# Two-layer float32 block, layer one's experts: residual rows kept in HBM, their tile a seventh home for gate and up weights, up and down homes given out apart

## What is computed

```python
mix = hybrid_mixer(a_in, w_in[l], ...)
h = h + gt1[:, None, :] * mix                 # residual rows
m_in = modulate(rmsnorm(h, norm2_g[l]), sh2, sc2)
moe = hier_moe(m_in, w_router_grp[l], w_router_exp[l], w_gate[l], w_up[l], w_down[l])
h = h + gt2[:, None, :] * moe
return rmsnorm(h, normf_g)

def hier_moe(h, ...):                         # 32 experts, two chosen per token, hidden width 256
    def expert_step(acc, ws):
        wg, wu, wd, gate_col = ws
        y = (jax.nn.silu(hf @ wg) * (hf @ wu)) @ wd
        return acc + gate_col[:, None] * y, None
```

## Time and profile before

| | us |
|---|---|
| median of 3 executions | 1344.69 |
| the profiled execution, its own time | 1346.78 |
| span of its trace | 1345.0 |
| TensorE busy | 1285.8 (96%) |
| VectorE busy | 651.4 (48%) |
| ScalarE busy | 338.0 (25%) |
| GpSimd busy | 272.8 (20%) |

### The profile page before, as it was taken

How to read it: one execution, slowest core, us unless ns; L and a number is a source line. 1 busy time by engine, 2 the same in 40 slices (tenths; PEclk the granted TensorE clock), 3 DMA queues, 4 the chain that set the end, 5 groups by cost and what they waited for, 6 DMA issues and landing times. The chain is left out here.

```text
span 1345.0 us, 20902 instructions
## 1 busy us (share of the span) xinstructions
PE 1285.8 (96%) x8436; PEld 749.6 (56%) x8436; DVE 651.4 (48%) x1325; ACT 338.0 (25%) x578; POOL 272.8 (20%) x376
## 2 busy tenths in 40 slices
PE   7999999999998987999999999999999999999997
PEld 3555678865456322333388888888864633333332
DVE  7739767546665321222579996143544522111007
ACT  5422342524012100101345564111001211111113
POOL 4100530001000110110137547905300001010000
PEclk8999999999998988999999999999999999999999
DMA  9910011356647999999933211312135679999994
GB/s 372 375 64 1 1 63 64 128 220 219 256 170 264 409 425 420 424 423 424 393 145 111 77 63 63 124 64 78 59 132 248 245 291 360 420 392 421 391 410 188
DMA packets 43826, 316.00 MB, mean 235 GB/s; under 512 B 7256, under 2 KB 7264, under 8 KB 25040
## 3 DMA queue, kind: packets, MB, share of 16 engines
q1 hardware_dynamic: 35688, 296.34, 55.2%
q0 software_dynamic: 7584, 17.23, 3.4%
q10 hardware_dynamic: 456, 1.08, 0.2%
HBM read 302.11 MB, written 22.56 MB: 241 GB/s over the span
## 5 line engine op out<-in xcount | busy, mean ns | idle before, releaser
L2481 PE MATMUL m_ps<-store,par 128*32 128x512 f32 (+2 forms) x896 | 148.6, 594 | 0.0
L2481 PE MATMUL mix_ps<-store,par 128*32 128x512 f32 (+2 forms) x608 | 122.0, 636 | 17.2 <-issue 8.1
L2369 POOL DMA_INDIRECT y_t<-x_rows,m_token x25 | 25.5, 1019 | 452.6 <-DVE m_token L2355 199.1
L3197 PE MATMUL mix_ps<-y_t,store 128*128 128x256 f32 x432 | 96.2, 379 | 0.0
L2625 DVE TENSOR_TENSOR m2r_a<-m2r_a,m_ps 128x256 f32<-128x256 f32 x22 | 9.3, 421 | 170.7 <-ACT m2r_a L2546 170.7
L2481 PEld LDWEIGHTS m_ps<-store,par 128*32 128x32 f32 (+2 forms) x896 | 46.0, 119 | 81.2 <-issue 81.2
L3197 PEld LDWEIGHTS mix_ps<-y_t,store 128*128 128x128 f32 x432 | 82.1, 190 | 13.7 <-issue 2.6
L1284 PE MATMUL mix_ps<-y_t,store 128*128 128x512 f32 x192 | 85.6, 599 | 0.0
L2481 PEld LDWEIGHTS mix_ps<-store,par 128*32 128x32 f32 (+2 forms) x608 | 38.2, 129 | 79.9 <-issue 79.7
L2503 PE MATMUL m_ps<-store,m2r_a 128*32 128x512 f32 (+2 forms) x448 | 76.3, 595 | 0.3 <-issue 0.2
L2503 PE MATMUL mix_ps<-store,m1r_a 128*32 128x512 f32 (+2 forms) x304 | 61.5, 619 | 7.4 <-issue 6.8
(11 more groups left out here) (848 smaller groups left out, 2426.3 us busy)
## 6 DMA issues: line engine op xcount, KB each, us to landing
store<-in_gu SPq DMA_DIRECT2D x51, 2048.0 KB, 15.8
store<-in_dn SPq DMA_DIRECT2D x51, 1024.0 KB, 18.1
store<-in_w_in SPq DMA_DIRECT2D x14, 2048.0 KB, 10.7
store<-in_w_ada SPq DMA_DIRECT2D x12, 2048.0 KB, 9.9
mods<-in_gu SPq DMA_DIRECT2D x8, 2048.0 KB, 17.0
store<-in_w_out SPq DMA_DIRECT2D x4, 2048.0 KB, 8.3
mods<-in_dn SPq DMA_DIRECT2D x8, 1024.0 KB, 21.2
store<-y_rows SPq DMA_DIRECT2D x8, 1024.0 KB, 10.2
```

The costliest lines, as they stand in the source:

```text
L2369: pool.indirect_dma_start(to, None, c.x_rows, bass.IndirectOffsetOnAxis(c.token[:, i:i + 1], 0), bounds_check=T - 1, oob_is_err=False).the ...
L2481: last = pe.matmul(ps[who, 2 + j % 2, :], xt[:, k, who], w[:, k, :], start=(k == 0), stop=(k == KD - 1))
L3197: last = pe.matmul(pz[:, bank, half_t[p]], left(p)[:, k, :], right[:, k, :], start=(k == 0), stop=(k == 3))
```

## The change

1. Layer one's residual rows are also stored in a new HBM tensor `x_home`, tile by tile in `mix_and_route.sync`, four DMAs of 512 KB (semaphore `put_by`).
2. `m.x` becomes home 6, a seventh, for up parts only. Unit 6's up part goes there in four pieces, before the loop of loads, after `put_by`.
3. Up and down parts have places of their own: `up_place` over seven homes, ties broken by the order (3, 4, 0, 1, 5, 2, 6), `down_place` over six as before.
4. `load_rows` brings `x_home` back to `m.x` in four DMAs of 512 KB, behind the norm rows and ahead of the wait for the scatters and of `y_rows`; the adds wait for both.
5. `keep_clock` in the router multiplies four 128-column pieces of `m.ident` in place of one 512-column piece of `m.x`. This and no more reaches layer two, whose homes stay six and whose order of loads stays.

```diff
+        self.x_home, self.NUP = x_home, NU if x_home is None else NU + 1
+        self.up_place, self.up_held = self.places(self.NUP, up_order, in_turn)
+        self.down_place, self.down_held = self.places(NU, range(NU), in_turn)
+    def places(self, count, order, in_turn):
+        place, held, holder = list(range(count)), {}, list(range(count))
+        for n in range(count, len(self.units)):
+            p = n % count if in_turn else min(order, key=lambda p: self.last[holder[p]])
+            held[n], holder[p] = holder[p], n
+            place.append(p)
+        return place, held
+    def up_pieces(self, n):
+        return SLOT // D if NU - 1 <= n < self.NUP or n in self.up_next(0) else 1
+    def down_pieces(self, n):
+        return (UNIT - SLOT) // D if n == NU - 1 or n in self.down_next(0) else 1
...
@@ mix_and_route, sync, in the loop over t @@
+            if c.x_home is not None:
+                sp.wait_ge(ev, 2 * t + 2)
+                sp.dma_start(c.x_home[t * P:(t + 1) * P, :], m.x[:, t, :]).then_inc(x.put_by, 16)
@@ keep_clock @@
-                pe.matmul(ps[:, bank, 0:n], m.ident[:], m.x[:, 0, 0:n], start=True, stop=True)
+                pe.matmul(ps[:, bank, 0:n], m.ident[:], m.ident[:, 0:n], start=True, stop=True)
-        keep_clock(1, HALF)
+        keep_clock(1, P, P, P, P)
@@ experts, sync @@
         load_up(sp, m, c, n, job)
         sp.wait_ge(x.order_r, 1)
+        if c.x_home is not None:
+            sp.wait_ge(x.put_by, 16 * NT)
+            load_up(sp, m, c, NU, job_of(NU))
         for j in range(NJ):
-            for n in c.next_in(j):
+            for n in c.up_next(j):
                 load_up(sp, m, c, n, job_of(n))
...
-                for n in c.next_in(j - 1):
+                for n in c.down_next(j - 1):
                     load_down(sp, m, c, n, job_of(n))
@@ load_rows @@
+    if c.x_home is not None:
+        for t in range(NT):
+            sp.dma_start(m.x[:, t, :], c.x_home[t * P:(t + 1) * P, :]).then_inc(c.back[t], 16)
     c.scattered(sp)
@@ add_rows @@
-    dve.wait_ge(c.back[t], 16)
+    dve.wait_ge(c.back[t], 16 if c.x_home is None else 32)
@@ program @@
+        m.up_at.append(m.x[:].rearrange("p t n -> p (t n)"))
```

More of the change, by code:

```diff
@@ L67, in __init__ @@
     def __init__(self, tag, NE, NG, EG, HV, F, runs, slots, early, later, router, bias, gu, dn, gate, x_rows, y_rows,
-                 got, stored, got_over, stored_over, gu_ready, dn_ready, up, down, back, KEPT, homes, in_turn):
+                 got, stored, got_over, stored_over, gu_ready, dn_ready, up, down, back, KEPT, homes, in_turn, x_home, up_order):
         self.tag, self.NE, self.NG, self.EG, self.HV, self.F = tag, NE, NG, EG, HV, F
@@ L105, in __init__, with up_slot, down_slot, up_landed @@
                 self.downs.append(count)
[L106 to L110, removed]
+        self.x_home, self.NUP = x_home, NU if x_home is None else NU + 1
+        self.up_place, self.up_held = self.places(self.NUP, up_order, in_turn)
+        self.down_place, self.down_held = self.places(NU, range(NU), in_turn)
         for j, pieces in enumerate(self.steps):
             for n, _ in pieces:
[L113 to L124, removed]
+                assert n < self.NUP or self.last[self.up_held[n]] < j
+                assert n < NU or self.last[self.down_held[n]] < j
+    def places(self, count, order, in_turn):
[5 more added lines that the diff above has]
+        return place, held
+    def up_slot(self, n):
+        return self.slots[self.up_place[n]]
+    def down_slot(self, n):
+        return self.slots[self.down_place[n]]
+    def up_pieces(self, n):
+        return SLOT // D if NU - 1 <= n < self.NUP or n in self.up_next(0) else 1
+    def down_pieces(self, n):
+        return (UNIT - SLOT) // D if n == NU - 1 or n in self.down_next(0) else 1
+    def up_landed(self, n):
+        return 16 * sum(self.up_pieces(k) for k in range(n + 1) if self.up_place[k] == self.up_place[n])
+    def down_landed(self, n):
+        return 16 * sum(self.down_pieces(k) for k in range(n + 1) if self.down_place[k] == self.down_place[n])
     def scattered(self, eng):
@@ L132, in free_for_last, with up_next, down_next @@
     def free_for_last(self):
-        j = max(self.last[n] for n in range(len(self.units)) if self.slot(n) in self.homes)
+        j = max(self.last[n] for n in range(len(self.units))
+                if self.up_slot(n) in self.homes + (NU,) or self.down_slot(n) in self.homes)
         assert j < len(self.steps) - self.HV
         return j
-    def next_in(self, j):
-        return [n for n in range(NU, len(self.units)) if self.last[self.held[n]] == j]
+    def up_next(self, j):
+        return [n for n, k in self.up_held.items() if self.last[k] == j]
+    def down_next(self, j):
+        return [n for n, k in self.down_held.items() if self.last[k] == j]
 def width_of(row):
@@ L1849, in load_up @@
 def load_up(sp, m, c, n, job):
-    s = c.slot(n)
-    if n >= NU:
-        sp.wait_ge(c.up, c.ups[c.last[c.held[n]]])
+    s = c.up_slot(n)
+    if n >= c.NUP:
+        sp.wait_ge(c.up, c.ups[c.last[c.up_held[n]]])
     src = c.gu[job] if isinstance(job, int) else c.gu[bass.ds(job, 1)].rearrange("o p n -> (o p) n")
-    pieces = c.pieces(n, SLOT)
+    pieces = c.up_pieces(n)
     w = SLOT // pieces
@@ L1861, in load_down @@
 def load_down(sp, m, c, n, job):
-    s = c.slot(n)
+    s = c.down_slot(n)
     if n >= NU:
-        sp.wait_ge(c.down, c.downs[c.last[c.held[n]]])
+        sp.wait_ge(c.down, c.downs[c.last[c.down_held[n]]])
     src = c.dn[job] if isinstance(job, int) else c.dn[bass.ds(job, 1)].rearrange("o p n -> (o p) n")
-    pieces = c.pieces(n, UNIT - SLOT)
+    pieces = c.down_pieces(n)
     w = (UNIT - SLOT) // pieces
@@ L2426, in sync @@
         sp.wait_ge(x.order_r, 1)
+        if c.x_home is not None:
+            sp.wait_ge(x.put_by, 16 * NT)
+            load_up(sp, m, c, NU, job_of(NU))
         for j in range(NJ):
-            for n in c.next_in(j):
+            for n in c.up_next(j):
                 load_up(sp, m, c, n, job_of(n))
             if j == 0 and HV == 1:
-                for n in c.next_in(0):
+                for n in c.down_next(0):
                     load_down(sp, m, c, n, job_of(n))
             if j > 1 or HV > 1:
-                for n in c.next_in(j - 1):
+                for n in c.down_next(j - 1):
                     load_down(sp, m, c, n, job_of(n))
@@ L2474, in up @@
                 for n in dict.fromkeys(n for n, _ in c.steps[j]):
-                    pe.wait_ge(c.gu_ready[c.slot(n)], c.landed(n, SLOT))
+                    pe.wait_ge(c.gu_ready[c.up_slot(n)], c.up_landed(n))
             for k in range(lo, hi):
@@ L2479, in up @@
                 for n, who in c.steps[j]:
-                    w = m.up_at[c.slot(n)].rearrange("p (k n) -> p k n", k=KD)
+                    w = m.up_at[c.up_slot(n)].rearrange("p (k n) -> p k n", k=KD)
                     last = pe.matmul(ps[who, 2 + j % 2, :], xt[:, k, who], w[:, k, :], start=(k == 0), stop=(k == KD - 1))
@@ L2493, in down @@
             for n in dict.fromkeys(n for n, _ in c.steps[j]):
-                pe.wait_ge(c.dn_ready[c.slot(n)], c.landed(n, UNIT - SLOT))
+                pe.wait_ge(c.dn_ready[c.down_slot(n)], c.down_landed(n))
             pe.wait_ge(hte, j + 1)
@@ L2501, in down @@
                     for n, who in c.steps[j]:
-                        w = m.down_at[c.slot(n)].rearrange("p (k n) -> p k n", k=2)
+                        w = m.down_at[c.down_slot(n)].rearrange("p (k n) -> p k n", k=2)
                         last = pe.matmul(ps[who, 6 + q, :], ht[:, k, who], w[:, k, q * HALF:(q + 1) * HALF],
@@ L2831, in behind @@
                 dve.wait_ge(again_in[t % 2], 16 * (t // 2 + 1))
+                if c.x_home is not None:
+                    dve.wait_ge(c.back[t], 32)
                 st.link(dve.scalar_tensor_tensor(row, again[:, t % 2, 0], x.weight[:, 1, t, 0:1], row, ALU.mult, ALU.add))
@@ L2840, in overflow, with load_rows @@
     return o
-def load_rows(sp, c, y):
+def load_rows(sp, m, c, y):
     rows = c.y_rows.rearrange("(k t p) n -> t p k n", k=2, t=NT)
+    if c.x_home is not None:
+        for t in range(NT):
+            sp.dma_start(m.x[:, t, :], c.x_home[t * P:(t + 1) * P, :]).then_inc(c.back[t], 16)
     c.scattered(sp)
@@ L2917, in early @@
         sp.dma_start(g_row, d["normf_g2"].partition_broadcast(P)).then_inc(g_in, 16)
-        load_rows(sp, c, y)
+        load_rows(sp, m, c, y)
     def sync(sp):
@@ L3832, in expert_semaphores @@
 def expert_semaphores(sem):
-    return dict(gu_ready=[sem(f"x_gu{n}") for n in range(NU)], dn_ready=[sem(f"x_dn{n}") for n in range(NU)],
+    return dict(gu_ready=[sem(f"x_gu{n}") for n in range(NU + 1)], dn_ready=[sem(f"x_dn{n}") for n in range(NU)],
                 up=sem("x_up"), down=sem("x_down"),
@@ L3860, in moe @@
         x.tr, x.xa, x.xd, x.chosen, x.order_r, x.exps = (sem(n) for n in ("tr", "xa", "xd", "tok", "ord", "ad"))
```

(6 more changed lines are left out.)

## The result

The changed kernel takes 1345.93 us, median of its executions, against 1342.29 for the kernel before; the ratio is 1.0024 with a 95% interval of 1.0014 to 1.0035, so 1.9 to 4.7 us slower. Two of its twenty executions took 1957.48 and 1896.95 us at a mean granted clock of 0.63 and 0.65; they are in that median, which is 1345.3 without them, and not in the ratio. The forecast was 2.8 us slower, within what one measurement can tell. The profiled execution took 1344.62 us with a span of 1342.9. (The medians of before come from more executions than the three shown ahead of the prediction.)

What follows compares the result with a forecast made beforehand. The prediction took a full DMA queue in layer one's experts (442 to 648 us, 422 GB/s) as the bound. -2.3 + 3.5 + 1.6 = +2.8 us on the median of 1344.69 gave 1347.5 us, range 1341.5 to 1351.5.

Steps and rivals of the forecast that it cites:

- (a): Layer one, 431 to 434 us: unit 6's up part fills the DMA gap, every later landing 2.3 us earlier.
- (b): Layer one's experts: unit 27's down part queues behind two up parts, delaying down(13), +3.5 us, or +1.2 with earlier start.
- (c): At down(13) in layer one's experts: matmuls behind its wait run slower at the lower clock level, +1.6 us.
- (d): Behind down(13), TensorE goes on as before; the last product of layer one's experts starts at 659.4 us.
- (e): End of layer one: x_home rows return before VectorE needs y_rows, hidden with 2.5 us to spare; 0, bound 2.6 us.
- (f): Layer one's four stores to x_home and the router's four small clock-keeping matmuls cost 0 us.
- The share: Layer one, 431 to 434 us: the DMA share, 0.25 before, would be near 1.
- the add without a DMA as its releaser: After layer one's experts: VectorE's first add, near 661 us, would not be released by a DMA.
- the first (the home pays in full): Layer one's experts: fewer TensorE waits, stage ends with its last byte, 2.5 to 4.8 us faster, 1340 to 1342; chance 0.2.
- The second: End of layer one: rows return too late for VectorE, +2.8 plus 2.6 to 4.3 us, 1350 to 1352; chance 0.2.
- The third: Layer one: last store to x_home lands after 428 us, earlier start lost, +5.1 us, 1349.8; chance 0.05.
- the one on bubbles and space: Repeating bubbles on TensorE can mean too little SBUF for the next tile; by it a seventh home would cure them.

Runs made afterwards that it cites:

- traffic_only: The changed kernel with six homes for up parts and the old load order, keeping the x_home stores, way back and new clock-keeping matmuls; 1.0036 to before.
- ctl_after: The changed kernel, unchanged, timed a second time as a control; ratio to the kernel before 1.0016.
- clock_x: The changed kernel with the one wide clock-keeping matmul of before in place of four narrow ones; ratio to the kernel before 1.0021.
- after_inter: The changed kernel with the x_home rows coming back tile by tile in turn with y_rows, nothing else; ratio to the kernel before 1.0032.
- down27_first: The changed kernel with unit 27's down part issued ahead of the up parts of 29, 30 and 31; ratio to the kernel before 1.0006.
- downs_first_inter: The changed kernel with down parts issued ahead of up parts from the third round on, and x_home rows interleaved with y_rows; 0.9982 to before, repeated 0.9986.

## Why the prediction was right, step by step

The size came out (2.8 forecast, 1.9 to 4.7 measured), and so did its place: the down part of 27, late behind the up parts of 30 and 31. But two terms of the sum were off and cancelled, which is luck, and the times on the trace were not those forecast. The means below are over four profiles with the old order (before, its two controls, traffic_only) and four with the new (changed, ctl_after, clock_x, after_inter), counted from the first router product; they spread by some 4 us each, so the terms are good to 1 or 2 us.

- **(a) the earlier start**, -2.3 forecast. Right, a little short. Unit 31's up part was there 289.5 us in in the first profile (issue plus landing) and let up(15) start 286.9, 285.6 and 286.9 us in in the three old profiles where it was the last thing waited for, mean 287.2; the down part of 27, now at that place in the queue, let down(13) start at 284.9, 282.8, 283.1 and 285.4, mean 284.0. That is -3.2. The share of 0.25 became 1.02, as forecast. The third of a microsecond set against it for one more part in pieces did not show: the stretch with the pieces moves at 410 GB/s, where before it moved 334. Why it was slower before is not shown; it moved only 352 GB/s from 438 to 440 us even at a share of 1.04.
- **(b) the order**, +3.5 forecast before the earlier start is taken off. The mechanism is shown by down27_first. The size was read from an execution whose down(13) began late: 286.0 us in, behind the longest router of the four, where the other three began at 282.0, 280.7 and 282.0. Against the mean of all four, 282.7, the term is 287.2 - 282.7 = +4.5.
- **(c) the clock behind the wait**, +1.6 forecast: 5.00, 5.35, 5.35 and 6.47 us for 3.65, so +1.9. That up(14) "paid" it before was true of the first profile alone.
- Sum of the means: -3.2 + 4.5 + 1.9 = +3.2. Router and experts together are 303.0 us with the old order and 305.5 with the new, +2.5; the rest is the wait of 0.9 us ahead of up(15), there in three of the four old profiles and gone in the new.
- **(d)** Right: behind down(13) no step waits for weights.
- **(e) the rows back**, 0, bound 2.6. Right for this kernel, and for the reason given: the first pair of y_rows was issued at 648.80 and landed 6.1 us later, at 654.9, 1.7 us ahead of the add (2.5 forecast). But the bound for an uncovered way back was too low: traffic_only shows 3.68 us at the add and 5.1 in the tail. It failed twice. Its DMAs ended as reckoned (the pair landed at 649.28 + 11.1 = 660.4, where the bound had 660.6), but VectorE was free at 656.7, as the experts ended earlier than in the first profile, from which 658.0 was read; and it ended at VectorE and left out TensorE's wait and slower matmuls behind it.
- **(f)** The stores and the four matmuls: 0, as clock_x and the lengths of router and experts in traffic_only show.

The signs. The share, the shorter waits at the last `up` steps, the longer ones at `down` steps, a wait ahead of down(13) (3.38 us for the 3 to 5 forecast; 2.08, 2.30 and 3.26 in the other three) and the add without a DMA as its releaser all came. The places in time did not: down(13) starts at 634.24 and not near 638, the product of the last rows at 655.20 for 659.4, the add at 656.59 for 661. By its own words, "I am wrong if down(13) starts by 635", the prediction failed this sign. 1.6 us of it is the head start of this execution; the rest is (a), larger than forecast, in a single profile that shows no loss. The loss of 3 us stands on the many executions and on the means. One sum of the prediction is wrong too: its "own range" of +0.5 to +4.5 is said to hold the bounds of (a), (c) and (e), but these reach to -1.0 + 3.5 + 3.4 + 2.6 = +8.5.

Of the rivals, the first (the home pays in full) did not come in this kernel; downs_first_inter comes near it: faster by 2 us where 2.5 to 4.8 was its price. The second was right in mechanism and wrong in place: it is not in the changed kernel, it is in the variants whose experts end earlier and whose rows do not go by turns. The third did not come: the pieces for `x` were issued at 426.40. Of the two rules weighed, the one on bubbles and space (the Trainium skill, "Perfetto Trace Analysis", Optimization Strategy) holds here in half: the home moved the waits and lengthened the longest of them, and paid only once the order was right. The landings of 1 and 2 MB weight parts that the runs show stayed in the order of issue, down to 634.15 for the down part of 27, so what the Trainium skill says in "DMA: Bandwidth & Descriptors", Queues, rings and completion order, did not decide anything here. It can be seen all the same: before, the first norm row, 512 KB, issued at 640.78, landed at 650.1, half a microsecond ahead of the down part of 31, issued at 623.96 (650.6).

What stays open: how the measured 3 us splits between (b) and (c), since no run changes one without the other, and why the clock holds in one execution and falls in the next.

## What to carry to other kernels

When a stage's DMA queue is always full, as it was here (422 GB/s before and after), one more buffer adds no rate: it only changes which part stands first, and how early. Write down the order of the last few transfers and ask for each what needs it and when; here one 1 MB part behind two of 2 MB that were needed later cost more than the buffer gave. And before a wait or a length from one profile goes into a sum, see whether it is there in a second one: the 8.77 us and the late down(13) were in one of four. The longest wait need not be the one that costs: the 12.7 us ahead of down(5) stayed when the loss went.

## What the runs showed of the hardware that was not expected

The granted clock in the router is not the same from one execution to the next, at the same instructions. The stretch from 412 to 416 us in the changed kernel and in ctl_after, the same program:

```profile
412.00:416.00 4.00, 4.00 (x20) 4.00 (x20) 2.88 (x16) 0.28 (x1) 0.00 (x0) 0.50 0.95 343
```

```profile
412.00:416.00 4.00, 3.26 (x29) 2.95 (x29) 3.37 (x20) 0.28 (x1) 0.00 (x0) 1.00 0.90 340
```

The clock is at 0.50, the lower level, in one and at 1.00 in the other. In both TensorE had idled 1.76 us just before, ahead of the matmuls for VectorE's `both`. The router takes 72.7 or 68.8 us accordingly. Part of that comes back in the experts, which wait for the same DMAs: down(13) starts 284.9 and 285.4 us after the first router product behind the two slow routers of the changed order, 282.8 and 283.1 behind the two quick ones, so some 2 of the 3.9 us are left there. The length of the experts alone does not show it: it is 233.1 and 235.2 us behind the slow routers, 235.2 and 235.6 behind the quick ones, as the matmuls of down(13) themselves took 5.00 us in the one and 6.47 in the other.
